# Routed experts computed two at a time, one of 128 and one of 64 slots, with their weight tiles interleaved by fours and twos

## The reference

```python
def moe_swiglu(xn, w_router, w_gate, w_up, w_down):
    xt = xn.reshape(-1, d)                                  # 256 x 1024
    logits = (xt @ w_router).astype(jnp.float32)            # 8 experts
    top_vals, top_idx = lax.top_k(logits, TOP_K)            # 2 of 8
    top_w = jax.nn.softmax(top_vals, axis=-1)
    combine = jnp.sum(jax.nn.one_hot(top_idx, N_EXPERTS, dtype=jnp.float32) * top_w[..., None], axis=1)
    for e in range(N_EXPERTS):                              # D_EXPERT = 3584
        y = y + combine[:, e:e + 1] * swiglu(xt, w_gate[e], w_up[e], w_down[e])
```

## Time and profile before

| | us |
|---|---|
| median of 3 runs (lowest, highest) | 2575.03 (2573.99, 2576.97) |
| the profiled execution, its own time | 2570.88 |
| its span, first to last instruction | 2569.1 |
| large experts, one turn | 119.2 |
| small experts, one turn | 108.3 |

### The profile page before, as it was taken

The page is one execution under the profiler, slowest core; times in us unless marked ns, Lnnn a source line. Parts: engine busy times, 40 slices in busy tenths (PEclk is TensorE's granted clock), DMA queues, the critical chain, the costliest instruction groups (busy, mean ns, idle before and its releaser), DMA issues.

```text
span 2569.1 us, 32438 instructions
## 1 busy us (share of the span) xinstructions
PE 2389.0 (93%) x12064; PEld 1866.2 (73%) x12064; DVE 2010.6 (78%) x3035; ACT 1257.4 (49%) x1302; POOL 288.0 (11%) x305
## 2 busy tenths in 40 slices
PE   9999999999999999999898898999999987778787
PEld 8899999899788888877677677888985543323332
DVE  5866754865888888989999998665668887787875
ACT  2554332364778777878888885316421111111111
POOL 0000000000000000000000000000013433333341
PEclk9999999999999999999999999999989999989899
DMA  7454654543799999999999997531769999999997
GB/s 245 157 189 133 196 191 142 163 158 123 297 376 380 369 388 373 382 374 414 414 415 409 414 416 248 155 98 54 235 246 416 421 421 421 421 422 422 422 421 298
DMA packets 238446, 786.10 MB, mean 306 GB/s; under 512 B 24368, under 2 KB 154544, under 8 KB 162288
## 3 DMA queue, kind: packets, MB, share of 16 engines
q1 hardware_dynamic: 198000, 504.46, 53.1%
q0 software_dynamic: 39184, 276.58, 26.4%
q10 hardware_dynamic: 1136, 3.43, 0.3%
HBM read 777.08 MB, written 7.34 MB: 305 GB/s over the span
## 4 chain that ended last, share of the span: by engine, by line
PE 60%; DMA 22%; DVE 8%; issue 5%; ACT 4%; POOL 0%; DVEq 0%; SPq 0%; ACTq 0%
DMA dense_weights<-in_peer_rows,work 15%; DMA weight_tiles<-in_moe_tiles 7%; PE banks L862 7%; PE banks L864 7%; PE banks L863 7%; PE banks L728 5%; PE banks L1327 5%; PE banks L682 5%; PE banks L683 5%; PE banks L686 5%; PE banks L660 4%; DVE weight_tiles_low L2584 3%; ACT weight_tiles_high L1858 2%; PE banks L592 1%; PE banks L968 1%
## 5 line engine op out<-in xcount | busy, mean ns | idle before, releaser
L2584 DVE TENSOR_TENSOR weight_tiles_low<-weight_tiles,weight_tiles_high 128x2048 fp32r<-128x2048 f32 x333 | 757.3, 2288 | 74.9 <-ACT weight_tiles_high L1858 70.0
L1858 ACT ACTIVATE weight_tiles_high<-weight_tiles 128x2048 fp32r<-128x2048 f32 x332 | 635.3, 1917 | 147.9 <-DMA weight_tiles<-in_moe_tiles 143.5
L1327 PE MATMUL banks<-dense_weights,work 128*128 128x512 f32 x888 | 411.9, 614 | 56.8 <-DVE work L3115 56.7
L1327 PEld LDWEIGHTS banks<-dense_weights,work 128*128 128x128 f32 x888 | 172.2, 198 | 287.8 <-issue 199.0
L3105 DVE CUSTOM_DVE_ANT_0 dense_weights<-dense_weights,banks 128x1024 f32<-128x1024 f32 x222 | 266.6, 1218 | 67.5 <-DMA dense_weights<-in_peer_rows,work 66.3
L2206 DVE TENSOR_TENSOR weight_tiles_low<-weight_tiles,weight_tiles_high 128x2048 fp32r<-128x2048 f32 x93 | 212.2, 2289 | 131.4 <-ACT weight_tiles_high L1625 131.2
L2120 ACT ACTIVATE work<-work,small 128x2 f32<-128x2 f32 x129 | 38.1, 295 | 538.1 <-DVE work L3105 537.8
L1601 POOL DMA_INDIRECT dense_weights<-in_peer_rows,work x222 | 209.1, 942 | 591.7 <-DVE work L3061 315.7
L968 PE MATMUL banks<-weight_tiles_high,gathered_parts 128*128 128x512 f32 x448 | 183.7, 410 | 27.5 <-DVE weight_tiles_low L2584 26.8
L1625 ACT ACTIVATE weight_tiles_high<-weight_tiles 128x2048 fp32r<-128x2048 f32 x93 | 177.3, 1909 | 57.5 <-PE banks L864 29.5
L682 PE MATMUL banks<-weight_tiles_high 128*128 128x256 f32 x800 | 190.5, 283 | 3.9 <-issue 3.1
(11 more groups left out here) (508 smaller groups left out, 4486.7 us busy)
## 6 DMA issues: line engine op xcount, KB each, us to landing
weight_tiles<-in_moe_tiles SPq DMA_DIRECT2D x336, 1024.0 KB, 7.5
weight_tiles<-in_w_in SPq DMA_DIRECT2D x38, 1024.0 KB, 5.5
weight_tiles<-in_w_xkv SPq DMA_DIRECT2D x16, 1024.0 KB, 5.7
weight_tiles<-in_ffn_w_gate SPq DMA_DIRECT2D x11, 1024.0 KB, 5.3
weight_tiles<-in_ffn_w_up SPq DMA_DIRECT2D x11, 1024.0 KB, 5.3
weight_tiles<-in_ffn_w_down SPq DMA_DIRECT2D x11, 1024.0 KB, 4.9
weight_tiles<-in_w_xq SPq DMA_DIRECT2D x8, 1024.0 KB, 5.2
weight_tiles<-in_w_xo SPq DMA_DIRECT2D x8, 1024.0 KB, 5.1
```

The source lines that it names most:

```text
L1327: mm = pe.matmul(halves[half], diag[(first + j) % 8], pair_row(first + j)[:, 1, half * 512:(half + 1) * 512], start=False, stop=end and j ...
L1858: act.activation(high_tile(j), raw_tile(j), ACT.Copy).then_inc(g.high, 1)
L2584: dve.tensor_tensor(low_tile(j), raw_tile(j), high_tile(j).bitcast(F32), ALU.subtract).then_inc(g.split, 1)
```

## The change

The eight turns become four pair turns, each of one large and one small expert (turn p has the experts of rank p and p + 4). The tiles of both go through the same ring in one order: four of the large expert's gate and up, four of the small one's, seven times; then two of the large one's down, two of the small one's, seven times; 84 tiles a turn. Tiles are numbered q in that order. The ring of rounded tiles has six buffers in place of seven (`EXP_RING`), since the small expert's output and two row buffers now stand in the seventh's room. The rounding of gathered tokens moves from DVE to ACT. `ranks()` moves ahead of the first token gather. The number of weight tiles, matmuls on them, roundings and subtractions is the same.

```diff
+PAIR_TILES = [(small, 4 * c + i) for c in range(CHUNKS) for small in (False, True) for i in range(4)]
+PAIR_TILES += [(small, GATE_UP + 2 * u + i) for u in range(CHUNKS) for small in (False, True) for i in range(2)]
+EXP_RING, FIRST_HIGH = RING - 1, RING - HIGH_RING - 1
+TOKENS_UNIT, HALF_TOKENS_UNIT = 1, 4
+TOKEN_STEPS = [2 * GATE_UP + 4 * TOKENS_UNIT + 5 + 2 * i for i in range(KT // 2)]
+HALF_TOKEN_STEPS = [2 * GATE_UP + 4 * HALF_TOKENS_UNIT + 5 + 2 * i for i in range(KT // 2)]
...
 # PE
-                    with pe.Fori(0, LARGE) as e:
-                        turn(e, False)
+                    with pe.Fori(0, PAIRS) as p:
+                        pair_turn(p)
...
+                    for c in range(CHUNKS):
+                        large_unit(c)
+                        if c >= 1:
+                            folded_transposes(c - 1)
+                        if c == LIST_CHUNK:
+                            slot_lists()
+                        small_unit(c)
+                        hidden_transposes(p, c)
+                        if c == HALF_LIST_CHUNK:
+                            half_lists()
...
+                        down_unit(False, u, large_halves)
+                        if u == 1:
+                            folded_transposes(CHUNKS - 1)
...
+                        down_unit(True, u, small_halves)
+                        if u == TOKENS_UNIT:
+                            token_transposes("gather", 16)
+                        elif u == HALF_TOKENS_UNIT:
+                            token_transposes("s_gather", 32)
+                    for key in ("gather", "s_gather"):
+                        pe.wait_ge(g.took_sems["v"], g.took[key, KT // 2 - 1] + p * g.takes["v"])
...
 # SP
-            sp.wait_ge(y_done, rows_added(N_EXP - 1))
+            sp.wait_ge(y_done, rows_added(PAIRS - 1, 1))
...
 # ACT, step q after the rounding of tile q + 4
+                        elif q in HALF_TOKEN_STEPS:
+                            token_high("s_gather", HALF_TOKEN_STEPS.index(q))
+                        if q == g.tiles - 2:
+                            outputs("down", "lists", ye, share_here)
+                    outputs("s_down", "s_lists", ye_half, share_half)
...
 # DVE, step q after the subtraction of tile q + 4
+                        elif q in HALF_TOKEN_STEPS:
+                            i = HALF_TOKEN_STEPS.index(q)
+                            half_low("s_gather", i, (p + 1) * (KT // 2) + i + 1)
```

More of the change, by code:

```diff
@@ L930, in gather, with gather_half @@
                         g.end(mm, (key, i))
-                def turn(e, small):
-                    g.begin_turn(e)
-                    gate_, up_, hidden_, lists_, gather_, down_ = (("s_" if small else "") + k for k in ("gate", "up", "hidden", "lists", "gather", "down"))
-                    def taken(who, key):
-                        pe.wait_ge(g.took_sems[who], g.took[key] + e * g.takes[who])
+                def gather_half(key):
+                    for i in range(KT // 2):
+                        bank = g.begin("v", (key, i))
+                        for j in range(2):
+                            for b in range(TB):
+                                mm = pe.matmul(bank[:, j * P:j * P + HALF], xT[:, b, (2 * i + j) * P:(2 * i + j + 1) * P],
+                                               pick_half[:, b, :], start=(b == 0), stop=(b == TB - 1))
+                        g.end(mm, (key, i))
@@ new lines, in mark, with hidden_transposes @@
+                def mark(mm):
+                    mm.then_inc(g.marked, 1)
+                    g.marks += 1
+                    g.used.append((g.marked, g.marks, g.per_marks))
+                def hidden_transposes(e, c):
+                    bank = g.begin("a", ("hidden", c))
+                    pe.wait_ge(g.took_sems["v"], g.took["up", c] + e * g.takes["v"])
+                    row = he[:, 0 if n == 0 else c % 2, :]
+                    for i in range(4):
+                        mm = pe.transpose(bank[:, i * P:(i + 1) * P], row[:, i * P:(i + 1) * P], ident[:, :])
+                    g.end(mm, ("hidden", c))
@@ new lines, in pair_turn, with split, both, folded_transposes @@
+                def pair_turn(p):
+                    g.begin_turn(p)
+                    def split(small, j, rows_):
+                        q = place_of(small, j)
+                        assert q == len(g.used)
+                        pe.wait_ge(g.split, p * g.tiles + q + 1)
+                        return (a.rearrange("p (k n) -> p k n", k=rows_) for a in (high_tile(q), low_tile(q)))
+                    def both(o, pairs, high, low, start, stop):
+                        pe.matmul(o, pairs, high, start=start, stop=False)
+                        return pe.matmul(o, pairs, low, start=False, stop=stop)
+                    def folded_transposes(c):
+                        bank = g.begin("v", ("s_hidden", c))
+                        for rows, key, at in ((he[:, 1, :], "s_gate", 0), (up_rows, "s_up", 4 * HALF)):
+                            pe.wait_ge(g.took_sems["a"], g.took[key, c] + p * g.takes["a"])
+                            for i in range(4):
+                                mm = pe.matmul(bank[:, at + i * HALF:at + (i + 1) * HALF], rows[:, i * P:(i + 1) * P], fold, start=True, stop=True)
+                        g.end(mm, ("s_hidden", c))
@@ new lines, in large_unit @@
+                    def large_unit(c):
+                        for n_, (who, name) in enumerate((("a", "gate"), ("v", "up"))):
+                            bank = g.begin(who, (name, c))
+                            for half in range(2):
+                                high, low = split(False, 4 * c + 2 * n_ + half, KT // 2)
+                                for i in range(KT // 2):
+                                    k = half * (KT // 2) + i
+                                    mm = parts(bank, xe_high[:, k, :], xe_low[:, k, :], high[:, i, :], low[:, i, :], k == 0, k == KT - 1)
+                                if half == 0:
+                                    mark(mm)
+                            g.end(mm, (name, c))
+                            g.used.append((g.group_done, g.total, g.in_turn))
@@ L1083, in _ @@
             skip_hint = pe.mark_branch_hint_location()
-            transposes("v", "put", [(b * P, weighted_now[:, b, :]) for b in range(TB)])
+            transposes("v", "put", [(b * P, weighted_half[:, b, :]) for b in range(TB)])
             pe.wait_ge(y_loaded, 16)
@@ L1482, in ranked_experts @@
+                for q in range(RING, g.tiles):
+                    pair_tile(g, 0, (0, at[PAIRS]), q)
+                    if q % RING == 0 and rest:
+                        r = rest.pop(0)
+                        at[r] = by_rank(r)
+                for p in range(1, PAIRS):
+                    for q in range(g.tiles):
+                        pair_tile(g, p, (at[p], at[PAIRS + p]), q)
                 return overflow
@@ L2619, in small_expert @@
[L2619 to L2626 removed]
+                    dve.tensor_copy(token, found[0:m, 0:1])
@@ L2659, in done, with expert @@
+                def expert(e, follow):
                     def done(key):
```

537 lines of the change are left out of this document (314 added, 223 removed).

## The result

The changed kernel takes 2601.03 us (median of 4 runs, 2600.01 to 2601.67), the kernel before 2574.51 us beside it: ratio 1.0102, 95 % interval 1.0084 to 1.0119. The change costs 26 us; I had forecast a gain of 19. The profiled execution took 2600.01 us with a span of 2598.2 us, 29.1 more than before.

A forecast was written before the change was run, and what follows sets the result against it. Transfers were to bound each pair, 221.2 us with pauses against 227.5. Experts ending 30 us earlier, less 10 at the end, took 2570.9 to 2551; plus 4.2 for the median, 2556, forecast 2545 to 2566, range 2537 to 2582.

The forecast's parts named there:

- Transfers bound a pair by 216.6 us, PE has 212: Whole pair turn: loads take 216.6 us, PE's work 212, at most 217.5, so the transfers set its length.
- Turn's end, PE stands 6 to 8 us: Between turns: PE waits 6 to 8 us for the small expert's last token part, behind the next turn's fourth tile.
- Low clock behind it, 1.6 us: After the turn-end wait: eight matmuls at the clock's lower level cost 1.6 us, bounds 0 and 3.4.
- Nothing inside the turn: Within the turn: PE leads for 56 tiles, transfers for 28; the two effects were set against each other.
- Hole in the stream, 3 us: At the turn's end: late-issued loads leave a gap in the transfers, priced at 3 us, bounds 1 and 6.
- Start, +1.3 us: Start of the experts: the second gather's matmuls and token part delay PE's first expert matmul 1.3 us, bounds 0 and 4.
- End, 10 us: After the last turn: PE waits for the last large expert's rows, then low clock; about 10 us lost.
- The sum of a turn: Pair turn: 216.6 of transfers, 3 for the hole and 1.6 for low clock make 221.2 us; the last 214.
- The third: Rival: the turn's end makes it slower, above 2580 us; PE stands 9 us, deciding at 226 a pair; chance 0.16.
- the first rival: Rival: the transfer stream never breaks, 217 us a pair, 2533 to 2545 us in all; chance 0.15.
- The fourth: Rival: HBM held to the rule's rate of about 358 GB/s, time 2630 us and more; chance 0.01.
- the signs of being wrong: Profile: transfers below 400 GB/s throughout, PE waits mid gate and up tiles, or a turn-end wait far from 7 us.

The follow-up runs named there:

- the repaired kernels: Changed kernel with token parts one tile apart, PE's loop written out and last fold earlier: 2559.73 us; variants with further edits, 2547.70 to 2559.45 us.
- The edit that removes it: Last large expert's rows put in by PE's matmuls, not added in DRAM; alone against the changed kernel: 2589.00 us, ratio 1.0075 to the kernel before.
- all edits: Changed kernel, PE's loop kept: token parts closer and awaited at first small tile, fold and ACT's output earlier, last rows by matmul: 2547.70 us, 0.9913.

## Why the prediction was wrong

The direction was wrong: 2556 forecast, 2601 measured. The step that failed is the turn's end: PE stands 13.8 us there and not 6 to 8, because behind the late token part it waits another 5.5 us for its own code, for which the sum has no term. With the wait moved behind the branch 24 of the 26 us come back. Against the profiled execution my sum was short by 49 us of span: experts' end 1578.9 where I had 1532 (47), and the end 12.9 us where I had 10 (3).

- **Transfers bound a pair by 216.6 us, PE has 212.** Right in its kind. PE's gate and up cycle of eight tiles takes 20.4 us (1390.46 to 1410.91) where I had 20.6, and in the repaired kernels the DMA share is 1.00 and the second and third turn take 221 to 225 us (the first, with no pause ahead of it, 215 to 219). So the 216.6 us of transfers were up to 8 us low for them; that alone would have left a gain, and it is not where the forecast failed.
- **Turn's end, PE stands 6 to 8 us.** This is the step that failed. Its mechanism is there and its piece is 8.4 us, 1.4 over my 7: ACT's copy of the large expert's output (1.25 us) stands ahead of the fourth tile's rounding, and my 4.7 us left it out. But what is late next was missing: PE's own instructions. The loop has no term in the sum; I did not ask whether a body of twice the length still stays. 5.5 us a turn, three times.
- **Low clock behind it, 1.6 us.** Twelve steps of 0.43 in place of 0.23 us are 2.4. Mis-sized by 0.8: the low stretch behind the longer pause is longer than the eight matmuls of the earlier trace rows.
- **Nothing inside the turn.** Wrong: 3.1 to 3.6 us at L1034, four times, with some 1.3 us of low clock behind each (six matmuls 0.43 apart from 829.0 to 831.3, and the transposes). In PE's order only two of the small expert's tiles now stand between the last fold and the token transposes, which take its bank next, and DVE reads the bank only behind its subtractions. I listed the fold's cost on PE and not who has to read its bank before PE gets it again.
- **Hole in the stream, 3 us.** It is there (0.84 and 0.87 of the share over the pause, 0.60 in its second piece), but counted by PE it is not a term of its own: PE's time and its pauses add up to the turn.
- **Start, +1.3 us.** 657.28 in place of 653.11, 4.2, of which 1.0 was there ahead of the experts (L956 at 647.19, L925 before at 646.21). The second gather's matmuls alone take PE 3.68 us (L969). Inside the bounds of 0 and 4.
- **End, 10 us.** Measured 12.9, with 7.14 for the addition (I had 6.5), 5.78 for the load (4.6) and the low clock on the transposes behind them. The edit that removes it shortens the end by 11.4 us in its trace (its own matmuls and transposes are the other 1.5) and the whole kernel by 7; the experts take 4 us longer in that trace, why is open. Right in its mechanism.
- **The sum of a turn.** My 221.2 was counted by transfers (216.6 + 3 + 1.6); counted by PE the same terms give 212 + 7 + 1.6 = 220.6. Measured 233.6, 13.0 more: 5.5 for instructions, 1.4 for the first piece over my 7, 3.2 for the bank, and 2.1 for the clock (0.8 and 1.3) make 12.2. These are lengths of pauses. Taken away one at a time they gave back less in time (the code 9 us of 16.5); that the transfers stand close behind would fit, but no run shows it. The last turn, with no pause at its end, took 220.9 where I had 214.
- **The rivals.** The third, slower by the turn's end, was the one that came, with the point from which it decides (226 us a pair) passed by 7.6; I had put it at 0.16 and a price of 9 us of standing. Against it I held that a nearly empty queue lands in 4.6 us; the load that the chain passes through at the turn's end takes 9.86 (867.84 to 877.70). The code is not in it either, so it had the sign right and half of the cause. In the first rival the text loses 10 us at the end and the sum adds 8; with 10 it is 2542 and not 2540. The fourth, an HBM limit of 358 GB/s (the Trainium skill, "DMA: Bandwidth & Descriptors", opening table), did not come: the pairs move 390 to 410 GB/s. Two of the signs of being wrong that I named came: a wait at the turn's end far from 7 us, and a rate below 400 GB/s in every stretch of the table above.

One thing stays open. In all 19 branches back with such a body that the traces have, the first matmul begins 1.7 to 1.9 us after a packet of q8 has landed, so the length of the pause is set by when that packet starts: 0.5 us before PE runs dry in the kernel before with a long loop, 1.5 to 1.7 us after it with all edits, 2.9 to 3.0 us after the token part in the changed kernel. Why it starts late is not shown; no run here separates the wait ahead of the branch from the load on the queues.

## What to carry to other kernels

Two loops merged into one have a body as long as both: look whether the instruction queue shows packets in every turn, and place PE's waits behind the branch, ahead of the first instruction that needs them, so that the fetch and the wait run beside each other. When steps are interleaved, follow each bank to its reader, and the reader to what stands ahead of it in its own order. A change that balances two limits shows its gain only when nothing stops both at once: here the same merged turn is 1.0 % slower with its waits in the wrong place, and 0.9 % faster with them moved and the end put right.

## What the runs showed of the hardware

- PE's code is fetched by DMA in 16 KB pieces. From 660 to 1130 us it took 4 packets where the loop's body stayed (the large turns before, none of them after 772 us) and 20 where it did not (that body doubled, or the pair turn), with a pause of 2.1, 4.4 or 5.5 us behind the branch.
- Behind each of those branches the first matmul began 1.7 to 1.9 us after one such packet had landed, 19 times out of 19. Written out without a loop, PE's code was read ahead across the turn's end, and PE started 0.1 to 0.2 us after what it waited for.
- Pauses of 4.4 us, three times, cost nothing that could be measured where the DMA share stayed at 1; 5.5 us, three times, behind a wait of 8.4, cost 9 us in sum where the share fell to 0.60.
- Sixteen transposes took 1.91 us at the clock's upper level and 3.60 at the lower one (granted clock 0.50 from 1583 to 1589 us), behind 10 us of standing still.
